# Shifting the operand buffers of a three-pass matmul kernel by 32 and 160 bytes

## The reference

```python
# first block, alpha = 2 ** 0.25
x = layer_norm(alpha * x + 0.5 * swiglu(x, w_gate, w_up, w_down))      # 1024 -> 2816 -> 1024
x = layer_norm(alpha * x + hybrid_mixer(x, ...))                       # three kinds of attention, gates, merged @ w_out
x = layer_norm(alpha * x + 0.5 * swiglu(x, w_gate, w_up, w_down))
# second block
u = rmsnorm(h) ; q, k, v, z, ... = split(u @ w_in)
h = h + rmsnorm((g_a * (gdn(...) @ w_a2d) + g_b * (nsa(...) @ w_b2d)) @ w_o)
f = causal_dwconv(rmsnorm(h) @ w_up) + bias ; f_gate, f_val = split(f)
h = h + rmsnorm((gelu(f_gate) * f_val) @ w_down)
h = h + rmsnorm((p @ w_ple) * sigmoid(h @ w_ple_gate))
```

## Time and profile before

| | us |
|---|---|
| median of 3 runs | 1125.18 |
| lowest, highest | 1123.74, 1125.71 |
| span of the profiled execution, first to last instruction | 1122.6 |
| PE busy / PEld busy | 1094.1 / 1023.2 |
| POOL busy | 902.3 |
| ACT busy / DVE busy | 621.2 / 495.1 |

### The profile page before, as it was taken

How to read it: one execution, slowest core, us unless ns; L and a number is a source line. 1 busy time by engine, 2 the same in 40 slices (tenths; PEclk the granted TensorE clock), 3 DMA queues, 4 the chain that set the end, 5 groups by cost and what they waited for, 6 DMA issues and landing times.

```text
span 1122.6 us, 22288 instructions
## 1 busy us (share of the span) xinstructions
PE 1094.1 (97%) x8110; PEld 1023.2 (91%) x8110; DVE 495.1 (44%) x904; ACT 621.2 (55%) x1002; POOL 902.3 (80%) x695
## 2 busy tenths in 40 slices
PE   8999999999999999999999999999999999999997
PEld 7999998999998998999999899889999798999985
DVE  4422113202456554421126655774766256454463
ACT  4444444654667866544443775555666565555564
POOL 6999996898664596999999589577355898999985
PEclk9999999999999999999999999999999999999999
DMA  7866665666342454766665466335233565666652
GB/s 244 282 204 193 187 195 165 206 222 192 115 131 78 130 184 139 230 202 198 192 182 181 135 193 188 118 116 159 65 94 127 183 202 172 180 197 187 189 184 77
DMA packets 52774, 191.29 MB, mean 170 GB/s; under 512 B 5856, under 2 KB 6112, under 8 KB 52320
## 3 DMA queue, kind: packets, MB, share of 16 engines
q1 hardware_dynamic: 50688, 182.47, 52.6%
q10 hardware_dynamic: 2016, 7.81, 2.1%
HBM read 189.21 MB, written 1.05 MB: 169 GB/s over the span
## 4 chain that ended last, share of the span: by engine, by line
POOL 51%; issue 27%; PE 19%; ACT 1%; POOLq 1%; DVE 1%; DMA 1%; SPq 0%; DVEq 0%; ACTq 0%
POOL weights_low L533 51%; PE banks L575 10%; PE acc L575 8%; DMA ring<-in_stream 1%; POOLq L539 0%; ACT weights_high L1440 0%; POOLq L530 0%; ACT tmp L1686 0%; ACT tmp L1956 0%; PE acc L749 0%; PE banks L766 0%; DVE act_buf L2016 0%; DVE res L2162 0%; POOL stat L547 0%; DVE xs L2174 0%
## 5 line engine op out<-in xcount | busy, mean ns | idle before, releaser
L533 POOL TENSOR_TENSOR weights_low<-ring,weights_high 128x512 fp32r<-128x512 f32 x686 | 899.2, 1345 | 208.7 <-ACT weights_high L1440 206.5
L1440 ACT CAST weights_high<-ring 128x1024 fp32r<-128x1024 f32 x343 | 356.1, 1047 | 216.4 <-PE banks L575 132.0
L575 PE MATMUL banks<-xT_high,weights_high 128*128 128x256 f32 x1264 | 351.5, 278 | 1.2 <-POOL weights_low L533 1.1
L575 PE MATMUL banks<-xT_low,weights_high 128*128 128x256 f32 x1264 | 350.3, 277 | 0.0
L575 PE MATMUL banks<-xT_high,weights_low 128*128 128x256 f32 x1264 | 350.3, 277 | 0.0
L575 PEld LDWEIGHTS banks<-xT_high,weights_high 128*128 128x128 f32 x1264 | 237.4, 188 | 4.2 <-issue 1.5
L575 PEld LDWEIGHTS banks<-xT_low,weights_high 128*128 128x128 f32 x1264 | 237.7, 188 | 2.3
L575 PEld LDWEIGHTS banks<-xT_high,weights_low 128*128 128x128 f32 x1264 | 237.9, 188 | 0.0
L1991 DVE TENSOR_TENSOR hf<-act_buf,banks 128x256 f32<-128x256 f32 x40 | 16.8, 421 | 225.2 <-ACT act_buf L1466 211.0
L575 PE MATMUL acc<-xT_high,weights_high 128*128 128x256 f32 x408 | 108.8, 287 | 1.8 <-ACT xT_high L1539 1.0
L575 PE MATMUL acc<-weights_high,hT_high 128*128 128x512 f32 x264 | 104.0, 394 | 2.2 <-issue 1.6
(11 more groups left out here) (362 smaller groups left out, 1577.5 us busy)
## 6 DMA issues: line engine op xcount, KB each, us to landing
ring<-in_stream SPq DMA_DIRECT2D x343, 512.0 KB, 3.7
rows<-in_big_rows ACTq DMA_DIRECT2D x3, 1024.0 KB, 8.2
rows<-in_big_rows ACTq DMA_DIRECT2D x3, 512.0 KB, 4.0
cst<-in_consts ACTq DMA_DIRECT2D x3, 470.5 KB, 4.8
xs<-in_x_tm ACTq DMA_DIRECT2D x2, 512.0 KB, 7.3
out<-xs SPq DMA_DIRECT2D x4, 256.0 KB, 2.1
gates<-in_x_fm SPq DMA_DIRECT2D x2, 256.0 KB, 4.2
ring<-in_stream SPq DMA_DIRECT2D x2, 256.0 KB, 4.3
```

Source lines behind the costliest of these rows:

```text
L533: last = nc.gpsimd.tensor_tensor(wlo[:, slot, hs], ring[:, slot, hs], whi[:, slot, hs].bitcast(F32), ALU.subtract)
L575: ins = nc.tensor.matmul(o, lhsT, rhs, start=start, stop=stop, **kw)
L1440: nc.scalar.copy(whi[:, ch % RING, :], ring[:, ch % RING, :]).then_inc(S["hi_ready"], 1)
```

## The change

Five lines of the allocation are changed or added; no instruction, wait or loop is. Each engine executes the same sequence of instructions as before, with other addresses.

```diff
-        sb("fill_stage", [144])
+        sb("fill_stage", [152])
+        sb("fill_hidden", [32], in_ffn)
         hT = pair("hT", [GROUP, T], in_ffn)
...
+        sb("fill_merged1", [32], block_one)
         mT1 = pair("mT1", [KD, T], block_one)
-        sb("pad1", [18 * T - 2 * KD * T], block_one)
+        sb("pad1", [18 * T - 2 * KD * T - 32], block_one)
...
+        sb("fill_merged2", [32], block_two)
         mT2 = pair("mT2", [KD, T], block_two)
+        sb("fill_turned", [96], block_two)
```

## The result

The change makes the kernel slower: 1129.18 us median of 6 runs (1128.32 to 1129.87), against 1124.85 us for the kernel before on the same chip (1123.74 to 1125.71, 6 runs). The ratio is 1.0036, with a 95% interval from 1.0025 to 1.0047: 4.3 us lost, where 9.1 were forecast as a gain. The profiled execution took 1129.17 us and its span is 4.7 us longer than that of before (1127.3 less 1122.6). In this and every other run 1.9 us lie outside the span; of the 2.6 us between the kernel before's median and its profiled span, the rest is the spread of its runs.

A forecast was written before the change was run, and what follows sets the result against it. PE was taken to bound the kernel, busy 97% of the span, with POOL some 6% behind in the loops. Gains 8.9 + 1.8 less 1.6 made 9.1 us: 1125.2 - 9.1 = 1116.1 us, range 1110 to 1124.

The forecast's parts named there:

- the main term: 512-column matmuls with hT or mT stationary, 984 moved from +96 to -64: 9 ns less each, 8.9 us gained.
- the xT matmuls: Gate and up, xT unmoved at -64: expected to stay at 113.0 ns a matmul, nothing counted in the sum.
- nothing gained: Upper bound for 512-column matmuls at -64: still 233.6 ns, since the second operand is the constantly written weights buffer.
- The middle value: 512-column matmuls: 228.9 ns, the cost read at +64, between the bounds 233.6 and 219.6 for -64.
- The rival that gave `down` nothing at all: Only the 256-column products gain, `down`'s excess coming from weights written while they stream: 1123.6 us, chance 11%.
- The 256-column term: 408 matmuls with oT and yT moving, brought to -64: from some 117.7 to 113.0 ns, 1.8 us gained.
- What gives back: Where POOL works without a pause, PE's saving becomes longer waits for `lo_ready`: 1.6 us of the gain lost.
- The five slow matmuls behind `down`: Five steps at 118 ns against 113.0 behind each `down`: might go, 1.6 us, counted only in the range.
- The rival that came true: the slow rhythm: `down` at -64 leaves gate and up at 117.5 ns: +14.0 us against -9.1, so 1130.1 us, chance 12%.
- point of decision: Slow rhythm outweighs `down`'s gain once over half the periods are caught: 48 followers lose 216 ns, twelve `down` matmuls win 108.
- The rule that spoke against it: Trainium skill: TensorE's two read ports are independent, so shifting operands is worth 0; as rival "nothing changes", 1125.2 us, chance 3%.

## Why the prediction was wrong, point by point

Two steps of the sum failed: the main term, which was almost all of the forecast gain and came out at nothing, and the xT matmuls, which the sum put at nothing and which cost 5.7 us, 4.8 of them behind a `down`.

**The main term, 984 x 9 ns = 8.9 us.** It took 224 ns for 512 columns at -64, from the excess of 6.3 ns that 256 columns have there. Measured: 232.9 for hT and 233.3 for mT, where +96 has 233.1 and 233.4. The gain was 0.2 ns for a matmul of hT (the 0.6 us of the account are mostly waits within the units at the ends of the layers: five steps of over 245 ns sum to 2.4 us before and 1.9 after), at the upper bound that the prediction had kept ("nothing gained"). The middle value that it named, 228.9 at +64, was the one that a run confirmed for hT, at +64 and not at -64: 229.1, and 229.0 for mT. The mistake was to carry a price over to another shape along an assumption (paid once for each weight load), when the only 512-column rows stood at +64; the nearest row was of the right shape at the wrong distance and would have given 4.6 us, still too much. The rival that gave `down` nothing at all, at 11%, was right about its size at -64 and wrong in its reason: an excess that comes from the weights being written, whatever the distance, doesn't go with hT's 229.1 at +64. And it knew nothing of what comes behind `down`.

**The 256-column term, 408 x 4.4 ns = 1.8 us.** Right in direction, too large. From the sums of all steps oT won 0.6 us and yT lost 0.1, under a third of it; without the steps lengthened by waits the gain is 216 x 3.1 + 192 x 2.0 ns = 1.1 us. The distance -64 gives oT and yT the same two rhythms as xT, and part of them runs in the slow one: oT from 396 to 402 us, yT up to 855 and again from 869 on. The timeline of the changed kernel, which answers to the earlier trace rows (first two rows and next two: branches; then mix):

```profile
397.07 0.28 PE L579 MATMUL banks<-oT_low,weights_high 128*128 128x256 f32 x1
...
400.95 0.28 PE L579 MATMUL banks<-oT_low,weights_high 128*128 128x256 f32 x1
...
406.05 0.28 PE L579 MATMUL banks<-oT_high,weights_low 128*128 128x256 f32 x1
...
409.00 0.28 PE L579 MATMUL banks<-oT_low,weights_high 128*128 128x256 f32 x1
...
855.80 0.28 PE L579 MATMUL banks<-yT_low,weights_high 128*128 128x256 f32 x1
...
859.43 0.28 PE L579 MATMUL banks<-yT_high,weights_high 128*128 128x256 f32 x1
```

33 steps in 3.88 us, 117.6; then 26 in 2.95, 113.5; 32 in 3.63, 113.4. So 117 to 118 at -96 is the rate that the kernel before has at that distance throughout, and 117.6 at -64 is the slow rhythm: two causes with nearly the same number, which the prediction's comparison of 113.0 with 117.3 could not tell apart.

**What gives back, 1.6 us.** Nothing, since there was no gain to give back. In gate, up and the mixers PE waited for POOL for 1.7 us before and 1.8 after (the list of waits: us in total, times, longest), and POOL's share in the middle of a layer is the same, 70.07 of 75 us (the last busy time in the row of the window) against the earlier trace rows:

```profile
PE banks L579 <- POOL weights_low L537: 1.8, 2, 1.1
```

```profile
500.00:575.00 75.00, 75.00 (x540) 70.15 (x540) 11.75 (x27) 31.07 (x36) 70.07 (x56) 1.00 0.63 193
```

**The five slow matmuls behind `down`.** They didn't go: in a fast stretch the first steps are 116, 118, 119, 116 ns and then 114 and 113, four slower steps where there were five. That is worth 0.01 us a stretch, the 0.3 us in the account above, and was rightly left out of the sum.

**The rival that came true: the slow rhythm, 12%.** It named the mechanism, the place and the time: rhythm inherited from what ran before, gate and up behind each `down`, 117.5 against 113.0, 1130.1 us. Its time came out 0.9 us from the measured one partly by luck. It let all of some 3100 matmuls be caught and let `down` win 8.9; measured were half of the stretches and a gain of 0.6. Its point of decision, "more than half of the periods", held only together with the gain in `down`; without that gain any slow period is a loss. Its ground against, that the fast rhythm is reached from `down`, transposes and attention alike, was drawn from a kernel in which hT stood at +96, where every `down` left the fast rhythm. I should have given it more: the prediction had seen in the earlier trace rows that the slow rhythm can stand for long behind a 512-column product, and the change altered precisely what runs ahead of 2592 matmuls. One reading in it was off: the slow rhythm of the earlier trace rows wasn't made by the z product at +64. It stands already ahead of z, in 192 matmuls from 645.09 us on, behind a single step of 0.22 us, and z left the slow rhythm as it found it.

**The rule that spoke against it.** The timelines show 113.4 ns for xT at -64 in the fast rhythm, 118.3 at -32 and 120.0 at -128, with a mean clock of 0.997 to 0.998 in all three kernels. By the Trainium skill, page "SBUF — State Buffer", section "Who interferes with whom", TensorE waits on no one and its two read ports are independent. Taken as saying that operand addresses are free, the rule disagrees with this case, and the measurement decides: 1.5 to 2.0% of the kernel hang on xT's place. For this change it would have given the better number (0, where +4.3 us came out and -9.1 were forecast), and for the wrong reason.

## What to carry to other kernels

Where one engine streams back to back, read the step from start to start by stretch and not by group: here two rhythms 4% apart hid in a mean duration that moved by 1 ns. A price of a placement holds for the shape and the neighbours where it was read; before a whole class is moved, one buffer alone is the cheap test. Where a rhythm is inherited, a change to one class can be paid by the class behind it, so count the followers first: here 792 matmuls were to win and 2592 stood behind them.

## What the runs showed of the hardware

- Back-to-back 256-column matmuls with a weight load each have two steady rhythms at a distance of -64, 113.4 and 117.8 ns, at the same granted clock (0.997 to 0.998 in the mean), and keep whichever they are in for at least 192 matmuls where nothing interrupts them. A single lengthened step can change it: 0.22 us at 644.87 us in the kernel before.
- Twelve 512-column matmuls at one distance keep the rhythm at +64 (34 fast, 17 slow) and flip it at -64 and +128; at +96 they left the fast one 51 times of 51, and never found the slow one. Eleven at -64 found and left the slow one. The 24 that open a layer don't always do what twelve do. With two distances mixed within the twelve the fast rhythm stood behind all of them in the seven kernels tried, whichever distance came last.
- 512 columns take 229.1 ns at +64 (but 233.3 in two openings of a layer), 231.5 at +128, 233.1 at +96 and 232.9 at -64; a mixture takes 231.6 to 232.6. 256 columns take 117.5 to 118.6 at -96, 118.3 at -32 and 119.5 to 120.0 at -128.
- All this is a description. Why the start addresses modulo 512 act so, and what holds the state, no run here shows; that it depends on the distance rather than on the absolute place was not tried by moving both operands together.
